# Quartered RMS sums, four modulation chunks moved a block later, unread products in two attentions, a later lambda

## The reference

```python
mod_x = ada_params(c, w_ada[l], b_ada[l])[:, None]
mod_c = ada_params(c_ctx, w_ada[l], b_ada[l])[None, None]
y = xf * lax.rsqrt(jnp.mean(xf * xf, axis=-1, keepdims=True) + NORM_EPS)      # rms_norm
h = modulate(rms_norm(x, g), mod[..., j, :], mod[..., j + 1, :])
return x + MACARON_W * mod[..., j + 2, :] * ((jax.nn.silu(gt) * up) @ w_down)
```

## Time and profile before

| | us |
|---|---|
| median of 3 runs (lowest, highest) | 2738.12 (2734.22, 2743.89) |
| the profiled execution | 2737.73 |
| its span in the trace | 2735.9 |
| TensorE busy | 2582.6 |
| VectorE busy | 1751.9 |
| ScalarE busy | 1082.4 |
| GpSimd busy | 136.4 |
| mean granted TensorE clock | 0.978 |

### The profile page before, as it was taken

The page is one execution under the profiler, slowest core; times in us unless marked ns, Lnnn a source line. Parts: engine busy times, 40 slices in busy tenths (PEclk is TensorE's granted clock), DMA queues, the critical chain, the costliest instruction groups (busy, mean ns, idle before and its releaser), DMA issues.

```text
span 2735.9 us, 41147 instructions
## 1 busy us (share of the span) xinstructions
PE 2582.6 (94%) x16148; PEld 2194.1 (80%) x16148; DVE 1751.9 (64%) x3301; ACT 1082.4 (40%) x2092; POOL 136.4 (5%) x92
## 2 busy tenths in 40 slices
PE   4869999899999999999998999999999999999999
PEld 3848998878888888887765788888788887777999
DVE  7567776667776765546678766654665543678754
ACT  2345545445443333323347333322433322445553
POOL 1000100000000011100000011100011100000010
PEclk9979999979999999999999999999999999999999
DMA  8926875915664344333610344434244434523653
GB/s 290 260 98 203 268 246 178 282 63 185 231 220 135 106 141 153 124 123 106 184 47 2 123 139 139 139 122 140 93 139 147 146 111 135 145 69 110 207 177 124
DMA packets 354891, 413.84 MB, mean 151 GB/s; under 512 B 24753, under 2 KB 291930, under 8 KB 354634
## 3 DMA queue, kind: packets, MB, share of 16 engines
q1 hardware_dynamic: 352496, 404.13, 46.0%
q0 software_dynamic: 1120, 5.70, 0.6%
q10 hardware_dynamic: 1082, 1.38, 0.1%
HBM read 409.56 MB, written 5.27 MB: 152 GB/s over the span
## 4 chain that ended last, share of the span: by engine, by line
PE 79%; DVE 11%; DMA 5%; ACT 3%; issue 2%; SPq 0%; ACTq 0%; DVEq 0%
PE bank L890 77%; DVE ada_partial L1575 4%; DVE weight_lo L686 2%; DMA raw_weights<-in_w_ffn_in_dram 2%; PE bank L1165 2%; DMA raw_weights<-in_w_in_ab_dram 1%; DMA raw_weights<-in_w_in_cd_dram 1%; ACT weight_hi L1251 1%; DVE bank L1877 1%; ACT H_hi L1343 0%; ACT X L1350 0%; DVE rstd L1824 0%; ACT probs L1468 0%; DVE bias L1828 0%; ACT tmp L1311 0%
## 5 line engine op out<-in xcount | busy, mean ns | idle before, releaser
L686 DVE TENSOR_TENSOR weight_lo<-raw_weights,weight_hi 128x512 fp32r<-128x512 f32 x1024 | 767.1, 757 | 832.1 <-ACT weight_hi L1251 818.6
L1251 ACT ACTIVATE weight_hi<-raw_weights 128x512 fp32r<-128x512 f32 x1024 | 632.6, 629 | 1276.3 <-PE bank L890 1163.9
L890 PE MATMUL bank<-H_hi,weight_hi 128*128 128x256 f32 (+1 forms) x2832 | 958.4, 338 | 35.6 <-DVE weight_lo L686 24.7
L890 PE MATMUL bank<-H_lo,weight_hi 128*128 128x256 f32 (+1 forms) x2832 | 939.9, 332 | 0.0
L890 PE MATMUL bank<-H_hi,weight_lo 128*128 128x256 f32 (+1 forms) x2832 | 939.2, 332 | 0.0
L890 PEld LDWEIGHTS bank<-H_hi,weight_hi 128*128 128x128 f32 x2832 | 541.4, 191 | 122.8 <-issue 53.9
L890 PEld LDWEIGHTS bank<-H_hi,weight_lo 128*128 128x128 f32 x2832 | 541.5, 191 | 50.7
L890 PEld LDWEIGHTS bank<-H_lo,weight_hi 128*128 128x128 f32 x2832 | 541.9, 191 | 47.7 <-issue 1.0
L1575 DVE SCALAR_TENSOR_TENSOR ada_partial<-raw_weights,silu_c,ada_partial 128x512 f32<-128x512 f32 x616 | 442.5, 746 | 1.3 <-DVE ada_partial L1575 0.2
L890 PE MATMUL bank<-hidden_hi,weight_hi 128*128 128x256 f32 (+1 forms) x1056 | 359.6, 340 | 4.8 <-DVE weight_lo L686 4.2
L890 PE MATMUL bank<-hidden_hi,weight_lo 128*128 128x256 f32 (+1 forms) x1056 | 355.6, 337 | 0.0
(11 more groups left out here) (184 smaller groups left out, 1992.7 us busy)
## 6 DMA issues: line engine op xcount, KB each, us to landing
raw_weights<-in_w_ada_dram SPq DMA_DIRECT2D x120, 1024.0 KB, 5.3
raw_weights<-in_w_ffn_up_dram SPq DMA_DIRECT2D x88, 1024.0 KB, 5.6
raw_weights<-in_w_ffn_in_dram SPq DMA_DIRECT2D x44, 1024.0 KB, 5.9
raw_weights<-in_w_ffn_down_dram SPq DMA_DIRECT2D x32, 1024.0 KB, 5.2
raw_weights<-in_w_in_dram SPq DMA_DIRECT2D x18, 1024.0 KB, 5.5
raw_weights<-in_w_ffn_out_dram SPq DMA_DIRECT2D x16, 1024.0 KB, 7.7
raw_weights<-in_w_in_ab_dram SPq DMA_DIRECT2D x12, 1024.0 KB, 9.5
raw_weights<-in_w_in_cd_dram SPq DMA_DIRECT2D x12, 1024.0 KB, 7.8
```

The source lines that it names most:

```text
L686: eng.tensor_tensor(WL[:, p.g % SPLIT, 0:p.kt * CW].rearrange("p (t n) -> p t n", n=CW), raw_ap(ch.n, ch.kt, CW)[:, p.k0:p.k0 + p.kt, :], ...
L890: return pe.matmul(o, w, x, start=start, stop=stop, skip_group_check=True)
L1251: act.activation(WH[:, p.g % SPLIT, 0:p.kt * CW].rearrange("p (t n) -> p t n", n=CW), raw_ap(ch.n, ch.kt, CW)[:, p.k0:p.k0 + p.kt, :], ACT ...
```

## The change

It does four things. (1) In the six RMS norms the sums of squares are made in quarters: a quarter of the columns each into a quadrant of 32 partitions, by a 32-column block of ones. Root and reciprocal then work on 128 partitions by a quarter of the columns; four products with a one-row operand spread each quarter over all partitions into banks 0 to 3 (`spread_rstd`), and VectorE and ScalarE copy two each to the tile rstd. `busy(34)` becomes `busy(10)`, the spread and `busy(18)`. (2) Steps 3, 5, 7 and 9 of w_ffn_in in the first block's second layer host no chunk. Four two-vector chunks are so taken up later: the same steps of the second block's first feed-forward take a second chunk each, behind u (`more`). (3) In the attentions of the first block TensorE does two unread products before each turn, save in two halves behind sub_sums of layer 0. (4) `lambdas` runs behind the first item of the first qkv projection, on both engines. The diff, without lines that only pass these on:

```diff
-    def __init__(self, g, u, host, gg, ug):
+    def __init__(self, g, u, host, gg, ug, more=None):
...
+    rstd_in, rstd_mm, rstd_cp = Tally(sem("rstd_quarters")), Tally(sem("rstd_spread")), Tally(sem("rstd_copied"))
...
-    def ffn(w_in, w_out, n, ada, gate, half, hosted, first):
+    def ffn(w_in, w_out, n, ada, gate, half, hosted, first, bare=(), twice=()):
         steps, host = [], hosted
         for s in range(NF // 2):
             g = chunk("g", view(w_in), 0, KC, CW * s)
-            a1 = ada_chunk() if host and len(ADA) < sum(ADA_CHUNKS) else None
+            a1 = ada_chunk() if host and s not in bare and len(ADA) < sum(ADA_CHUNKS) else None
             u = chunk("g", view(w_in), 0, KC, DFF + CW * s)
-            steps.append(Step(g=g, u=u, host=a1, gg=group("act"), ug=group("dve")))
+            more = ada_chunk() if s in twice else None
+            steps.append(Step(g=g, u=u, host=a1, gg=group("act"), ug=group("dve"), more=more))
...
-        add("proj", n=n, groups=groups, ada=ada, gate=gate, half=half, hidden=True, first=first,
+        add("proj", hosted=len(ADA) if bare else None, n=n, groups=groups, ada=ada, gate=gate, half=half, hidden=True,
+            first=first,
...
-    ffn(a["w_ffn_in"][1], a["w_ffn_out"][1], T, 1, 5, False, True, True)
+    ffn(a["w_ffn_in"][1], a["w_ffn_out"][1], T, 1, 5, False, True, True, bare=(3, 5, 7, 9))
...
-        ffn(a["w_ffn_up_2"][l, 0], a["w_ffn_down_2"][l, 0], n, 2 + l, 2, True, True, False)
+        ffn(a["w_ffn_up_2"][l, 0], a["w_ffn_down_2"][l, 0], n, 2 + l, 2, True, True, False,
+            twice=() if l else (3, 5, 7, 9))
...
                 load(at, lambda k: s.steps[k].u)
+                if s.steps[at.u].more:
+                    load(at, lambda k: s.steps[k].more)
...
                 features(at, lambda k: s.steps[k].u, s.steps[at.u].ug, KC, 0, HH, HL, s.n)
+                if s.steps[at.u].more:
+                    ada(at, lambda k: s.steps[k].more)
...
         def squares(s, t, bank):
             pe.wait_ge(stat_in.sem, s.stat_in + t + 1)
-            mm(bank[:, 0:s.n], ones[:, :], T1[:, t % 2, 0:s.n], t == 0, t == NT - 1).then_inc(stat_mm.sem, 1)
+            if s.kind == "rms":
+                w = s.n // 4
+                for q in range(4):
+                    ins = mm(bank[32 * q:32 * q + 32, 0:w], ones[:, 0:32], T1[:, t % 2, w * q:w * q + w], t == 0,
+                             t == NT - 1)
+                ins.then_inc(stat_mm.sem, 1)
+            else:
+                mm(bank[:, 0:s.n], ones[:, :], T1[:, t % 2, 0:s.n], t == 0, t == NT - 1).then_inc(stat_mm.sem, 1)
+
+        def spread_rstd(s):
+
+            pe.wait_ge(rstd_in.sem, s.quarters + 1)
+            w = s.n // 4
+            for q in range(4):
+                mm(BANK[q][:, 0:w], ones[32 * q:32 * q + 1, :], RB[32 * q:32 * q + 1, 0:w], True, True
+                   ).then_inc(rstd_mm.sem, 1)
...
-            busy(34 if s.kind == "rms" else 20)
+            if s.kind == "rms":
+                busy(10)
+                spread_rstd(s)
+                busy(18)
+            else:
+                busy(20)
 
         def attn(s):
+            def busy(h, n):
+
+                after_sub = s.sub and h.n in (s.sub[1] + 1, s.sub[1] + 2)
+                for _ in range(n if h.nb < 4 and h.vrow == D and not after_sub else 0):
+                    mm(B_T[h.cp % 2][:, 0:P], ident[:, :], ones[:, :], True, True)
...
                     score(hs[i + 2])
+                busy(h, 2)
                 turn(h)
...
-            act.activation(RB[:, 0:s.n], bank[:, 0:s.n], ACT.Sqrt, bias=eps, scale=1.0 / D).then_inc(rstd_sq.sem, 1)
+            w = s.n if s.kind == "ln" else s.n // 4
+            act.activation(RB[:, 0:w], bank[:, 0:w], ACT.Sqrt, bias=eps, scale=1.0 / D).then_inc(rstd_sq.sem, 1)
+            if s.kind == "rms":
+                act.wait_ge(rstd_mm.sem, s.spread + 4)
+                for q in (2, 3):
+                    act.activation(RB[:, w * q:w * q + w], BANK[q][:, 0:w], ACT.Copy).then_inc(rstd_cp.sem, 1)
...
                 ins.then_inc(ev_act.sem, 1)
+                if s.layer == 0 and i == 0:
+                    lambdas()
...
-                if s.kind == "mod":
-                    lambdas()
...
-                chain.link(dve.reciprocal(RB[:, 0:n], RB[:, 0:n]))
+                if not rms:
+                    chain.link(dve.reciprocal(RB[:, 0:n], RB[:, 0:n]))
+                else:
+                    w = n // 4
+                    dve.reciprocal(RB[:, 0:w], RB[:, 0:w]).then_inc(rstd_in.sem, 1)
+                    dve.wait_ge(rstd_mm.sem, s.spread + 4)
+                    for q in (0, 1):
+                        ins = dve.tensor_copy(RB[:, w * q:w * q + w], BANK[q][:, 0:w])
+                    chain.link(ins)
+                    if n == T:
+                        dve.wait_ge(rstd_cp.sem, s.copied + 2)
...
+                        if t == 0 and v:
+                            dve.wait_ge(rstd_cp.sem, s.copied + 2)
...
-                ahead_of(at, lambda k: s.steps[k].u)
+                ahead_of(at, lambda k: s.steps[k].u, (lambda k: s.steps[k].more) if s.steps[at.u].more else None)
...
-                if s.kind == "mod":
-                    lambdas()
...
+                    if s.layer == 0 and i == 0:
+                        lambdas()
```

4 lines of the change are left out of this document (3 added, 1 removed).

## The result

The changed kernel takes 2698.57 us (median of 4 runs, 2697.97 to 2699.28) where the kernel before, run beside it, takes 2741.01 (4 runs, 2734.22 to 2745.22): a ratio of 0.985, 95% interval 0.983 to 0.987, so 1.5% faster. The forecast was 2693 us in a range of 2676 to 2717. The two profiled executions took 2699.28 and 2737.73 us, 38.5 apart, and their spans, 2697.4 and 2735.9, differ by as much. All that follows compares points of these two traces.

The account below looks back on a forecast made before the run. TensorE was taken as the bound (79% of the chain, VectorE 11%). From 2737.7 us: moved chunks -18, norms -22.5, unread products -6, lambda +1.5, giving 2692.7, about 2693 us, range 2676 to 2717.

Parts of the forecast that it names:

- the ring's load: w_ffn_in, layer 1: a 5.70 us weight load waiting for a modulation chunk's raw slot, predicted to leave the chain from step 3.
- cost the same in both places: Column sums of the four moved chunks, predicted to cost equally in either block, so the move itself costs 0.
- 10.9, close under TensorE: VectorE's work in a hosted w_ffn_in step, summed from pieces, weight_lo and tmp: 10.9 us against TensorE's 11.44.
- I take TensorE ... 11.7: w_ffn_in, layer 1: TensorE sets the pace at 11.7 us a step, eight steps in 93.6 us against 112.5.
- for the thin slack: Margin on the moved chunks: 18 of the predicted 18.9 us gain kept, VectorE being close under TensorE.
- rival 3: Norms: quarters do not overlap behind a full product, or the spread is dear; -5 instead of -22.5, 2710 us, chance 0.07.
- Three pairs a norm inside a TensorE-bound projection: Three norms: 0.95 us saved on each of three squares pairs, 2.85 us a norm.
- busy(10) is 2.2 us, done before the reciprocal: RMS norms: the unread products ahead of the spread take 2.2 us and end before VectorE's reciprocal.
- rival 6: Less TensorE work drops the clock in each norm, costing 8.9 us a norm; ends over 2746 us, chance 0.03.
- half the way: Unread products in both attentions: taken between clock rising and not, -4 layer 0 and -2 layer 1, -6 us together.
- rival 1: The clock comes up in both attentions: -16.5 in place of -6, 2682 us, chance 0.19.
- The load after next: First qkv projection: chunk and weight loads starting at 60.92 us, predicted some 0.8 us later with lambda moved; term +1.5.

Follow-up runs that it names:

- e4_norms_back: The changed kernel with the six RMS norms as in the kernel before (all columns, 34 unread calls): 2716.9 us, ratio 0.990 to the kernel before.
- e5: The kernel before with only the two unread products ahead of each attention turn added: 2728.1 us, ratio 0.995 to the kernel before.
- e2: The changed kernel without the unread products in the two attentions: 2718.1 us, ratio 0.990 to the kernel before.
- e1: The changed kernel with the four modulation chunks back in steps 3, 5, 7 and 9 of w_ffn_in, layer 1: 2712.5 us, ratio 0.988.
- a_again: The changed kernel run once more, nothing edited: 2698.6 us, ratio 0.985 to the kernel before.
- e7: The changed kernel with eight unread calls ahead of each round of the third layer's query/key norm: 2701.9 us, ratio 0.986 to the kernel before.
- e12_dose1: The changed kernel with one unread call in place of two ahead of each first-block attention turn: 2708.8 us, ratio 0.989 to the kernel before.
- e13_norm_fill: The changed kernel with seven more unread calls ahead of the last squares pair in five RMS norms: 2696.6 us, ratio 0.985 to the kernel before.

## Why the prediction was right, and where its steps were not

The total came within 6 us, and that closely by luck, since the errors of the steps cancel. Two parts were priced too high by some 5 and 3 to 4 us, one too low by 1 to 13, and 4.3 us went where none was looked for.

**Part 1, moved chunks: -18 forecast, -12.9 measured (13.75 in w_ffn_in, less 0.85 in the second block).** The mechanism is as told: the ring's load left the chain in all eight steps, and the second block took the chunks for no more than their column sums. That they "cost the same in both places" missed that these lay under VectorE's steps before and lie on TensorE's path now. The step that failed is the sum for VectorE, "10.9, close under TensorE", and with it "I take TensorE ... 11.7". It lacked what the chain of after shows: ScalarE's hidden_hi ahead of the weight_hi that VectorE waits for, 1.3 us from the end of tmp to the next weight_lo, the fold of 0.24, and one more weight_lo behind the last accumulation. With these it is 11.9 us to TensorE's restart with two weight_lo of the step still to do, and every second hosted step stands still for 2.0 us. The other hosted steps are TensorE's, 11.54 and one column sum of 0.93 with its switch, and the bare ones 11.54. So 8 x 11.54 + 2 x 0.93 + 2 x 2.0 = 98.2, measured 98.4, against the 93.6 of the prediction. The range for the part, 9 to 19, held it. The 0.9 us kept back "for the thin slack" were too few.

**Part 2, norms: -22.5 forecast; -19.6 by the stages, -18.4 by the medians.** The new pair is 0.78 us, where 0.77 was forecast, the reciprocal 0.95 as worked out from the earlier trace rows, the chain behind it 1.27 us (end of the reciprocal at 1242.63 to 1243.90) and not 1.4. That the quarters overlap is settled, and with it rival 3. Two steps failed. "Three pairs a norm inside a TensorE-bound projection": the third pair isn't, since TensorE stands still behind it anyway, until ScalarE has the last squares, and the 0.95 us saved only make that standstill longer (1.88 us where it was 0.93). Two pairs save 2.2 us (the first stands right behind column sums of the same form and saves 1.3, the other 0.9), and the rest of the 4.0 is the exposed end, 1.8 where 1.6 was forecast. And "busy(10) is 2.2 us, done before the reciprocal" fails in the first norm, where the clock is at 0.50 from 858 to 860 us and comes up only while these passes run: they take from 859.91 on 2.9 us, the reciprocal ends at 861.47 and the spread starts at 862.81. The trace of the changed kernel has it (timeline of all engines):

```profile
860.52 0.95 DVE L1727 RECIPROCAL rstd<-rstd 128x128 f32<-128x128 f32 x1 [6.05 <-ACT rstd L1366]
...
862.81 0.50 PE L898 MATMUL bank<-rstd,ones 1*128 1x128 f32 x8
```

That norm gave 2.9 us in e4_norms_back and 1 to 3 over all traces, and not 4.4. The last gave 1.1 where 1.0 was forecast.

The difference of the stages to the medians, 1.2 us, may be rival 6, in small. It said that with less work on TensorE the clock falls in each norm; it does fall, in 10 of 32 quartered norms, 1.6 us each, 1.2 times an execution, 2 us. It was given a chance of 0.03 as a thing of 8.9 us a norm (17.8 us at half clock), and at that size it was wrong; as a cost inside the part it belonged in the sum.

**Part 3, unread products: -6 forecast; -6.7 between the two profiled executions, -11.7 alone (e5), -19.5 taken back (e2).** Here the forecast was a mean of two worlds, "half the way", and the traces show only one of them: the clock comes up in both attentions, rival 1's mechanism, each time that two calls are there. Left at half way, the term was mis-sized. The prediction's argument against it, that TensorE had been busy for 14 of 14 us at 0.50 without a rise, did not hold. The Trainium skill (TensorE: Matmul & The Clock Gate, Part 1) says that sustained activity releases the throttle. In direction e5 and e2 agree: with two calls ahead of each turn the granted clock is at 1.00 from 7 to 11 us into the attention of layer 1 on, in all ten traces that have them, with none it can stay at 0.50 for 52 us. By the busy time that the profile shows they don't, since TensorE is busy for 50.9 of these 52 us. Why the first 14 busy us of the kernel before were not enough stays open; a busy time of 14 of 14 comes from modelled ends of matmuls, so short gaps between them may be missing from it.

Rival 1's price was off too, in the way that counts for the profiled pair: it halved all busy time at 0.50. A pair of forgetting halves goes from 8.39 us to 4.91, 41% and not 50% (why not by half was not looked into), the first 7 to 11 us of the attention still run at half clock for the most part, and the calls cost 0.76 a pair. So -9.5 for layer 1 became -3.2 against this execution of before. And the measure itself moves: the one trace of the kernel before has a stretch at 1.00 where e2 has none, and the runs of the kernel before spread: beside e1 to e4 their mean granted clock goes from 0.971 to 0.977 while their time goes from 2752 to 2736 us. With the unread products alone (e5) it is 0.985 to 0.989 in seven runs, and they lie within 6.5 us. A single profile was the wrong base for this term; its own size runs from 7 to some 18 us.

**Part 4, lambda: +1.5 forecast, nothing that can be told.** The load after next starts at 61.12 instead of 60.92, so the order of events is as described, but the three loads that follow take 12.5, 10.8 and 9.2 us against 11.2, 11.4 and 12.1, and such differences cover the term.

**Not in the forecast:** the fall of 4.3 us at 2350 in the profiled execution. It comes and goes between executions of one kernel (a_again doesn't have it). At that wait or in the products behind it six of the nine traces with quartered norms and without e7's blocks show a fall (four of 4.5 us and two of 1.5), and none of the three with the norms of before. Whether the change makes it likelier, or three are too few, stays open.

The parts by these measures sum to 12.9 + 19.6 + 11.7 = 44.2 us, lambda at zero; less some 2 for the falls in the norms, 42.2, against 42.4 between the medians. That they meet so well is chance in part, since the third term moves with the execution.

## What to carry to other kernels

When an engine is predicted to be just under the one that sets the pace, write down its whole cycle from the trace's chain, with the hand-overs through other engines and what it does once a group, before calling it hidden: 10.9 us against 11.7 became 11.9 and a stall of 2. Where work is taken off TensorE beside a standstill, look at the granted clock of the stage over several executions, and fill the standstill with unread products only where TensorE waits anyway; count how many places the edit reaches. A statistic that is the same on every partition can be kept in quarters through root and reciprocal, and spread at the end: some 4 us in each of four norms here, 1 to 3 in the first and 1 in the last, which is half as wide.

## What the runs showed that was not expected

The granted clock of one stage differs between executions of the same kernel: the norms at 1240 and 1527 us in a_again and not in the first profile, the wait at 2350 the other way round. With less than two unread calls the differential halves of layer 0 stay at 1.2 GHz with TensorE busy for 17.2 of 20 us (e12_dose1), and with two the clock is up for most of them at 16.9 (the changed kernel): the busy share of a window doesn't tell which it will be. Two calls don't fix the moment either: in e13_norm_fill the clock comes up only some 18 us into layer 0, which takes 55.3 us. Filled, none of 12 norms falls; that 13 calls are the least number needed was not tried.

One-row products onto four banks cost 0.50 us for eight passes at full clock. Onto one bank, each product behind a wait for the one before, sixteen take 3.81, at full clock too. A reciprocal costs 0.95, 1.75 and 3.35 us for 128, 256 and 512 columns, and 3.34 for 512 columns on 64 partitions, so columns alone count.
